# Second block of a three-block kernel: narrower waits, one row tile's ties moved into the attention, the gate product moved ahead of the gating unit

## The reference, cut to what matters

```
proj = x @ w_in + b_in            # a_u a_v a_g | bq bk bv bg | cq ck cv cg | iq ik iw | mq mg
ya = gelu(a_u) * (W_s LN(gelu(a_v)) + b)          # spatial gating, blocks of 128 positions
yb = chunk_band_attention(bq, bk, bv)             # each 64-chunk sees itself and 8 before
# yc: for each query the 256 best keys by an index score, then attention over those keys
score = sum_h relu(iq_h . ik / 8) * iw_h / sqrt(8)     # masked to earlier and own chunks
_, idx = top_k(score, 256);  yc = softmax attention over k[idx], v[idx]
ym = softmax(mq . km) vm                          # 256 memory tokens
y  = [ya*silu(a_g), yb*silu(bg), yc*silu(cg), ym*silu(mg)] @ w_out + b_out
out = layer_norm(alpha * x + y)
```

## Time and profile before

| | |
|---|---|
| timed runs | 2763.82, 2764.42, 2764.93 us |
| span of the profiled execution, first to last instruction | 2763.9 us |
| PE busy | 97% of the span |
| DVE busy | 75% |
| ACT busy | 39% |
| POOL busy | 17% |
| index scores begin, search begins, attention begins (us from the start) | 1135, 1223, 1459 |

### The profile page before, as it was taken

The page is one execution under the profiler, slowest core; times in us unless marked ns, Lnnn a source line. Parts: engine busy times, 40 slices in busy tenths (PEclk is TensorE's granted clock), DMA queues, the critical chain, the costliest instruction groups (busy, mean ns, idle before and its releaser), DMA issues.

```text
span 2763.9 us, 33573 instructions
## 1 busy us (share of the span) xinstructions
PE 2689.4 (97%) x13192; PEld 2199.6 (80%) x13192; DVE 2086.6 (75%) x2796; ACT 1069.2 (39%) x1599; POOL 477.0 (17%) x254
## 2 busy tenths in 40 slices
PE   6999999999999999999999999999999999999998
PEld 5888888888888878778875678888887888888887
DVE  6999998873724663369998886688186988887978
ACT  5111112243413332245537751365232554555332
POOL 0000000000100002001210001354211656655000
PEclk8999999999999999999999999999999999999999
DMA  5312222224325452011101032100132222225431
GB/s 223 116 63 69 94 97 61 84 92 142 99 107 175 136 176 90 31 62 39 47 30 36 32 123 96 46 31 23 62 115 80 96 77 89 87 77 188 170 99 61
DMA packets 97710, 250.18 MB, mean 91 GB/s; under 512 B 7361, under 2 KB 34369, under 8 KB 96018
## 3 DMA queue, kind: packets, MB, share of 16 engines
q1 hardware_dynamic: 93010, 231.49, 24.4%
q10 hardware_dynamic: 4288, 15.73, 1.5%
q0 software_dynamic: 256, 0.82, 0.1%
HBM read 202.92 MB, written 45.09 MB: 90 GB/s over the span
## 4 chain that ended last, share of the span: by engine, by line
PE 80%; DVE 14%; issue 2%; ACT 1%; DMA 1%; DVEq 0%; ACTq 0%
PE pair L370 16%; PE pair L372 16%; PE pair L371 16%; PE pair L3657 7%; PE pair L3242 5%; PE pair L3244 5%; PE pair L3245 5%; DVE counted L1942 3%; PE pair L2593 2%; DVE reached L1993 1%; PE pair L2156 1%; DVE top_i L1999 1%; PE pair L1754 1%; PE pair L2172 1%; PE pair L2185 1%
## 5 line engine op out<-in xcount | busy, mean ns | idle before, releaser
L370 PE MATMUL pair<-u_hi,w_hi 128*128 128x512 f32 x768 | 302.1, 393 | 1.2 <-PEq L92 0.9
L641 DVE SCALAR_TENSOR_TENSOR conv_acc<-aT,cols,conv_acc 128x1024 f32<-128x1024 f32 x232 | 297.9, 1284 | 6.7
L371 PE MATMUL pair<-u_lo,w_hi 128*128 128x512 f32 x768 | 300.3, 391 | 0.0
L372 PE MATMUL pair<-u_hi,w_lo 128*128 128x512 f32 x768 | 300.3, 391 | 0.0
L370 PEld LDWEIGHTS pair<-u_hi,w_hi 128*128 128x128 f32 x768 | 145.2, 189 | 32.7 <-issue 2.4
L371 PEld LDWEIGHTS pair<-u_lo,w_hi 128*128 128x128 f32 x768 | 145.0, 189 | 30.6 <-issue 0.7
L372 PEld LDWEIGHTS pair<-u_hi,w_lo 128*128 128x128 f32 x768 | 145.0, 189 | 30.6
L370 PE MATMUL pair<-h_hi,ch_hi 128*128 128x512 f32 x392 | 153.8, 392 | 2.8 <-ACT ch L1824 2.6
L372 PE MATMUL pair<-h_hi,ch_lo 128*128 128x512 f32 x392 | 152.7, 389 | 0.0
L371 PE MATMUL pair<-h_lo,ch_hi 128*128 128x512 f32 x392 | 152.6, 389 | 0.0
L1014 POOL TENSOR_TENSOR yrT<-yrT,gate_c 128x1024 f32<-128x1024 f32 x8 | 18.9, 2366 | 758.1 <-ACT yrT L907 758.1
(11 more groups left out here) (510 smaller groups left out, 7105.1 us busy)
## 6 DMA issues: line engine op xcount, KB each, us to landing
wt<-in_w_ch SPq DMA_DIRECT2D x60, 512.0 KB, 3.4
wo_raw<-in_w_out SPq DMA_DIRECT2D x44, 512.0 KB, 3.6
wt<-in_w_up SPq DMA_DIRECT2D x10, 1024.0 KB, 4.9
w_raw<-in_w_up SPq DMA_DIRECT2D x10, 1024.0 KB, 4.8
g_spill<-g_stage SPq DMA_DIRECT2D x40, 256.0 KB, 2.2
ada_mod<-in_ada_mod SPq DMA_DIRECT2D x4, 2048.0 KB, 14.3
wt<-in_w_conv SPq DMA_DIRECT2D x16, 512.0 KB, 3.5
qk<-qk_st SPq DMA_DIRECT2D x8, 1024.0 KB, 6.4
```

Of the source, the lines that this page charges most:

```text
L370: nc.tensor.matmul(bank, w[0], x[0], start=(first and k == 0), stop=False)
L371: nc.tensor.matmul(bank, w[0], x[1], start=False, stop=False)
L372: return nc.tensor.matmul(bank, w[1], x[0], start=False, stop=(last and k == n_k - 1))
L641: nc.vector.scalar_tensor_tensor(dst, x, w, conv_acc[:], ALU.mult, ALU.add).then_inc(conv_step, 1)
```

## The change

1. PE starts the index logits when six of the eight row tiles have left PSUM, not all eight (`row_ok`).
2. ACT runs a one-element Silu ahead of the relus, so that the function table of channel 5's evacuation is in place.
3. PE does the first half of channel 7 between the transposes of the memory and the products that need them; the second half follows the memory values.
4. Channels 19 to 24 use the pairs 3, 2, 0, 1, 3, 2 in place of 2, 3, 0, 1, 2, 3; channel 18 sits in pair 2.
5. Row tile 7's six tie instructions leave the stretch before the attention and stand one each at the end of items 20 to 25.
6. POOL multiplies gelu(a_u) by silu(a_g) in place, ahead of channel 13's low part, and DVE's `gate_product` waits for that; SP copies the result to `mixedT` by two DMAs (once the channels are done), where POOL's two products in the attention stood.

```
-        N_TIES, TIES_AHEAD = 6 * (TT - 2), 36
+        N_TIES, TIES_AHEAD, TIES_FROM = 6 * (TT - 2), 30, 20
-        CH_PAIR = [2, 0, 3, 1, 2, 4, 0] + [n % 4 for n in range(7, SGU_AT)] + [2, 3, 0, 1, 2, 3]
+        CH_PAIR = [2, 0, 3, 1, 2, 4, 0] + [n % 4 for n in range(7, SGU_AT)] + [3, 2, 0, 1, 3, 2]
...
         def mix_gpsimd(pool):
             for n in range(N_CH):
+                if n == 13:
+                    pool.wait_ge(ch_out, 11)
+                    for c in range(2):
+                        u = chT[chan("a_u", c)][:]
+                        nc.gpsimd.tensor_tensor(u, u, chT[chan("a_g", c)][:], ALU.mult).then_inc(a_gated, 1)
                 pool.wait_ge(ch_hi, n + 1)
...
-            pool.wait_ge(ch_mm, N_CH)
-            for c in range(2):
-                pool.wait_ge(mixed_ok, 2 + 4 * c)
-                pool.wait_ge(a_mul, c + 1)
-                nc.gpsimd.tensor_tensor(mixedT[:, c, :], chT[chan("a_u", c)][:], chT[chan("a_g", c)][:],
-                                        ALU.mult).then_inc(a_mixed, 1)
...
             pe.wait_ge(ch_out, 5)
-            pe.wait_ge(row_ok, TT)
+            pe.wait_ge(row_ok, 6)
...
+            pe.wait_ge(row_ok, 2 * TT)
+            channel(pe, 7, 0)
             pe.wait_ge(memT_ok, 2)
...
-            pe.wait_ge(row_ok, 2 * TT)
-            for n in range(7, SGU_AT):
+            channel(pe, 7, 1)
+            for n in range(8, SGU_AT):
...
+            nc.scalar.activation(silu_ahead[:], eps6[:], ACT.Silu)
             for n, (t, g) in enumerate(logits):
...
             def gate_product(c):
                 dve.wait_ge(a_mm, c + 1)
-                dve.wait_ge(ch_out, 9)
+                dve.wait_ge(a_gated, c + 1)
...
-            sp.wait_ge(a_mixed, 2)
+            sp.wait_ge(a_mul, 2)
+            for c in range(2):
+                sp.dma_start(mixedT[:, c, :], chT[chan("a_u", c)][:]).then_inc(a_mixed, 16)
+            sp.wait_ge(a_mixed, 32)
...
-                if TIES_AHEAD + n < N_TIES:
-                    tie_operation(dve, TIES_AHEAD + n)
+                if 0 <= n - TIES_FROM < N_TIES - TIES_AHEAD:
+                    tie_operation(dve, TIES_AHEAD + n - TIES_FROM)
```

More of the change, by code:

```diff
@@ L109, in build @@
         exp_ahead = at(4.21875, "exp_ahead", [P, 1])
+        silu_ahead = at(4.25, "silu_ahead", [P, 1])
         wt = at(5, "wt", [P, 2, KT, P])
@@ L1628, in build @@
         a_b_bc = at(133, "a_b_bc", [P, MEM])
-        a_in, a_gelu, a_sd, a_mv, a_v_ok, a_mm, a_own, ws_ok, a_mul, a_mixed = (sem(x) for x in (
-            "a_in", "a_gelu", "a_sd", "a_mv", "a_v_ok", "a_mm", "a_own", "ws_ok", "a_mul", "a_mixed"))
+        a_in, a_gelu, a_sd, a_mv, a_v_ok, a_mm, a_own, ws_ok, a_mul, a_mixed, a_gated = (sem(x) for x in (
+            "a_in", "a_gelu", "a_sd", "a_mv", "a_v_ok", "a_mm", "a_own", "ws_ok", "a_mul", "a_mixed", "a_gated"))
         st6a = small3[:, 0:48].rearrange("p (t s) -> p t s", s=6)
```

## The result

| | before | changed |
|---|---|---|
| first comparison, 20 runs each, us | 2764.76 (2763.64 to 2766.35) | 2770.78 (2764.70 to 2775.65) |
| again on another chip, 16 and 11 runs | 2765.22 (2764.61 to 2767.39) | 2766.17 (2764.46 to 2770.51) |
| again on a third, 21 and 11 runs | 2766.37 (2764.68 to 2767.62) | 2767.74 (2765.35 to 2772.87) |

The ratios are 1.002 (95% interval 1.0015 to 1.0026), 1.0007 (0.9998 to 1.0016) and 1.0009 (1.0 to 1.0017). The forecast was 2764.1, with a range of 2759.0 to 2767.2: wrong. The changed kernel is slower in the first comparison by 0.2%; in the third its interval begins at 1.0, and the second is undecided. Its own runs spread over 6 to 11 us, where those of before spread over 3.

The account below looks back on a forecast made before the run. DVE was taken to set the attention's start, PE with ACT 0.9 behind. Earlier attention -3.5, products gone -2.4 and ties +5.6 gave -0.3 on the median 2764.42: 2764.1 us, range 2759.0 to 2767.2.

Parts of the forecast that it names:

- the 2.64: PE's wait ahead of channel 19 in the kernel before, forecast to go by the new choice of pairs.
- The gating: PE's spatial gating between channels 18 and 19; its work was taken as unchanged.
- the wait: PE stands ahead of the spatial gating until ACT has evacuated channel 17, at 1383.96 - s.
- Rival B: Tie scan in item 21 opens a PE gap over 2.29, TensorE's clock falls: +1.3, 2765.7 us; chance 0.17.
- the logits' fall: Clock drop behind PE's 2.11 gap at row tile 4's index logits; costs 1.56, forecast to go with the shorter gap.
- Lead (s): Before the search: search, memory load and channels all start 3.6 us earlier (bounds 0 to 3.6).
- X: In the search: POOL's two gate products stop DVE for their whole length, 4.8 us (bounds 0 to 4.8).
- PE's arrival: PE reaches the spatial gating at 1379.19 - s and waits there.
- Attention's start: First exponent at about 1459.3 - s, so the attention begins 3.5 us earlier.
- Products gone from the attention: POOL's two products leave the attention, saving 1.21 each, 2.4 us in all (bounds 0 to 3.0).
- Ties: Row tile 7's six tie instructions in attention items 20 to 25 cost 5.6 us (bounds 3.8 to 7.0).

Follow-up runs that it names:

- the filled version: The whole change, with PE's wait for channel 17 ahead of the spatial gating filled by nine matmuls whose results are not read: 2764.33 us, on another chip 2764.63.

## Why the prediction was wrong

The step that failed: "From there to the last channel the work is unchanged but for the 2.64." The gating in that stretch took 10.79 in the first profile (9.14 to 10.79 in five), where the sum had it at its 7.6. The prediction found the wait and its cause, and took it for a delay only. It did not ask what the clock would do in the work behind it: there it would have had to set its own row, 2.11 of waiting and a clock of 0.57 behind it, beside a new wait that it put at 4.8. It leaned on the one gap that drew no fall, 2.64 in front of full-width matmuls. Rival B had the mechanism, but at the scan, where the gap on PE was 1.60 and not over 2.29, DVE paces and a fall costs 0.2; and its price, the 1.56 of the logits' fall, is what the mildest fall in the gating cost; the others cost up to 5.6. The first comparison's median is 6.0 above the kernel before; no profile of the changed kernel shows that much, and what its longest runs do stays open.

Step by step, in the profiled execution:
- Lead (s): 3.6 forecast, 4.6 measured by the Gelu; in the other profiles with edits 1 and 2 the Gelu lies between 1217.7 and 1220.3, a lead of 2.9 to 5.6 over the one profile of before. With edit 6 alone it stands at 1222.46. Right.
- X: 4.8 forecast, (2.32 - 0.17) + (3.45 - 1.34) = 4.26 measured. No semaphore stands between these instructions and POOL's products, so the engines do not meet at semaphores alone. The Trainium skill, page "SBUF — State Buffer", section "Who interferes with whom", has VectorE and GpSimd share a pair of ports, held for a whole instruction by whoever issued first, and a two-input VectorE instruction among those that need it; the update of 2.32 agrees.
- PE's arrival: 1379.19 - s forecast. With s = 4.6 that is 1374.6; PE was there at 1378.97 - 2.03 = 1376.94, 2.4 later. Channel 13's low part ends at 1306.85 + 2.40 = 1309.25 and its matmuls start at 1309.30; channel 14's at 1320.53 and 1320.59. From one start to the next it is 11.29 for a channel of 16 x 0.68 = 10.88: channel 13 began 0.2 late, and 14 to 18 lost 0.4 each. The delay of DVE goes by ACT's sums and high parts to POOL, and not by channel 17's evacuation alone. This step was missing; with the smaller X it shortened the wait from 4.8 to 2.0.
- The gating: 7.6 forecast by silence, 10.79 measured. Attention's start: 1459.3 - 3.6 = 1455.7 forecast, 1457.74 measured, the difference nearly all in the gating (+3.2, less 1.4 for its earlier start).
- Products gone from the attention: -2.4 forecast, -2.27. Ties: +5.6 forecast, +5.0. Right: with edit 6 undone the memory items are 2.3 longer, and with the ties back ahead what follows them is 4.8 shorter.

Without the fall the rest of the sum stands within 1.1 to 1.4: the filled version is 1.4 and 1.7 below the kernel before on its two chips, 0.3 was forecast. The smaller X and the cheaper ties are on that side. What the fall costs differed between the comparisons: the changed kernel's median is 6.0, 1.0 and 1.4 above the kernel before. The second median, 2766.17, lies inside the range, though its profile has the fall as well; there the number would have been right by luck, with the step as wrong.

## What to carry to other kernels

A new wait of TensorE is priced with the work behind it: if that work may run at half clock, its length is added, and with small matmuls behind the wait it was longest here. Before a producer is moved into a search that other engines follow, walk the whole ring of waits (DVE, ACT's sums, ACT's high part, POOL's low part, PE), not only the one that stands last. A wait that can't be avoided is cheaper filled with matmuls than left idle; better is to take away what makes it, here one evacuation placed ahead of two sums.

## What was unexpected

With a wait of 0.2 us the runs fell into two groups 5 us apart (0.17 with a fall, 0.20 without); with no wait the slower group was absent from ten runs. The same program had half-level stretches of different lengths from run to run. And versions without any wait at the gating still had falls at the attention's start in some executions and not in others. The Trainium skill, page "TensorE: Matmul & The Clock Gate", section "HAM oscillation — how this bites in real kernels", says that a gap re-throttles TensorE and that the next work starts cold; the five profiles of the changed kernel agree (half level behind 2.03 to 2.08). That a gap of 2.64 in the kernel before drew no fall stays unexplained, as does what sets the length of a fall.
